# A fused two-block transformer step: transposed inputs from the host, splits on one engine, and a reordered second mixer

## The reference

```python
h = rmsnorm(x, mix_pre_g)                       # first block
u, v_s, q, k, v_a, g_a, g_b, f = split(h @ w_in)
y_a = spatial_gating(gelu(u), gelu(v_s), ...)
y_b = forgetting_attention(q, k, v_a, f, b_forget)
x = x + rmsnorm((sigmoid(g_a) * y_a + sigmoid(g_b) * y_b) @ w_out, mix_post_g)
x = x + rmsnorm(swiglu(rmsnorm(x, ffn_pre_g), w_gate, w_up, w_down), ffn_post_g)
proj = rmsnorm_2(x, norm_mix_g) @ w_in_2        # second block
x = x + concat(pool_mixer, mlstm_mixer, attn_mixer) @ w_out_2
x = x + mem_cross_attn(rmsnorm_2(x, norm_mem_g), mem, ca_wq, ca_wkv, ca_wo)
x = x + ec_moe(rmsnorm_2(x, norm_ffn_g), router_w, expert_w_gu, expert_w_down)
return rmsnorm_2(x, final_norm_g)
```

## Time and profile before

| | |
|---|---|
| median of 3 runs (lowest to highest) | 1486.63 us (1486.63 to 1488.58) |
| profiled execution | 1486.36 us, of which 1484.6 us are the profile's span |
| PE busy | 1147.1 us, 77% |
| DVE / ACT / POOL busy | 468.4 / 398.3 / 74.1 us |
| DMA | 503.33 MB, mean 339 GB/s |
| x and first products | to 25.3 us |
| first block | to about 426 us |
| second block with its mixer and router | to about 588 us |
| experts and final norm | to the end |

### The profile page before, as it was taken

The page is one execution under the profiler, slowest core; times in us unless marked ns, Lnnn a source line. Parts: engine busy times, 40 slices in busy tenths (PEclk is TensorE's granted clock), DMA queues, the critical chain, the costliest instruction groups (busy, mean ns, idle before and its releaser), DMA issues.

```text
span 1484.6 us, 19383 instructions
## 1 busy us (share of the span) xinstructions
PE 1147.1 (77%) x8336; PEld 754.3 (51%) x8336; DVE 468.4 (32%) x954; ACT 398.3 (27%) x890; POOL 74.1 (5%) x89
## 2 busy tenths in 40 slices
PE   9999999999999998995566466566665564565677
PEld 7888988888877875442322223223222232232234
DVE  6575777656788764110000000000000000000002
ACT  5665567555657642110000000000000000000002
POOL 0000020000035411000000000000000000000000
PEclk9999999999999998798778778787887787887789
DMA  8435546555553488999999999999999999999996
GB/s 313 171 138 203 198 172 223 208 207 199 199 187 114 149 347 343 397 436 434 433 437 426 433 433 435 424 442 430 430 437 426 438 430 433 433 426 440 423 424 288
DMA packets 29450, 503.33 MB, mean 339 GB/s; under 512 B 4275, under 2 KB 4915, under 8 KB 8245
## 3 DMA queue, kind: packets, MB, share of 16 engines
q1 hardware_dynamic: 25344, 493.43, 79.7%
q10 hardware_dynamic: 4020, 8.66, 1.6%
HBM read 501.03 MB, written 1.05 MB: 338 GB/s over the span
## 4 chain that ended last, share of the span: by engine, by line
issue 60%; PE 32%; DVE 5%; ACT 1%; POOL 1%; POOLq 0%; DVEq 0%; ACTq 0%
PE PB L378 9%; PE PB L358 5%; PE PB L359 5%; PE PB L360 5%; PE PB L379 4%; DVE SPL L1575 1%; DVE XN L1595 0%; PE PB L409 0%; POOL SP L2238 0%; PE PB L815 0%; PE PB L680 0%; PE PB L418 0%; PE PB L507 0%; PE PB L799 0%; PE PB L454 0%
## 5 line engine op out<-in xcount | busy, mean ns | idle before, releaser
L919 PE MATMUL PB<-RING,XS 128*32 128x512 f32 x2048 | 292.8, 720 | 177.0 <-DMA RING<-in_wgu_dram 176.7
L919 PEld LDWEIGHTS PB<-RING,XS 128*32 128x32 f32 x2048 | 68.4, 126 | 345.3 <-issue 249.8
L951 PE MATMUL PB<-RING,HHT 128*32 128x256 f32 x2048 | 150.9, 452 | 111.9 <-DMA RING<-in_wdn_dram 110.5
L1575 DVE TENSOR_TENSOR SPL<-RAW,SPH 128x512 fp32r<-128x512 f32 x318 | 207.0, 709 | 31.4 <-ACT SPH L1048 28.7
L378 PE MATMUL PB<-XT,SPH 128*128 128x512 f32 x544 | 194.1, 401 | 0.0
L1048 ACT ACTIVATE SPH<-RAW 128x512 fp32r<-128x512 f32 x340 | 186.8, 620 | 7.4 <-DMA RAW<-in_wst_dram 3.3
L951 PEld LDWEIGHTS PB<-RING,HHT 128*32 128x32 f32 x2048 | 75.3, 129 | 172.2 <-issue 141.7
L379 PE MATMUL PB<-XT,SPL 128*128 128x256 f32 x544 | 152.4, 280 | 0.0
L1506 ACT ACTIVATE SG<-PB 128x512 f32<-128x512 f32 x16 | 9.6, 597 | 506.1 <-PE PB L919 506.1
L2128 DVE SCALAR_TENSOR_TENSOR YL<-PB,COLS,YH 128x256 fp32r<-128x256 f32 x64 | 31.0, 484 | 279.0 <-ACT YH L1520 279.0
L378 PEld LDWEIGHTS PB<-XT,SPH 128*128 128x128 f32 x544 | 102.2, 188 | 24.6
(11 more groups left out here) (398 smaller groups left out, 1577.5 us busy)
## 6 DMA issues: line engine op xcount, KB each, us to landing
RAW<-in_wst_dram SPq DMA_DIRECT2D x84, 1024.0 KB, 4.9
RING<-in_wgu_dram SPq DMA_DIRECT2D x13, 2048.0 KB, 40.4
RING<-in_wgu_dram SPq DMA_DIRECT2D x4, 4096.0 KB, 22.3
RING<-in_wgu_dram SPq DMA_DIRECT2D x14, 1024.0 KB, 8.1
RING<-in_wdn_dram SPq DMA_DIRECT2D x6, 2048.0 KB, 13.4
RING<-in_wdn_dram SPq DMA_DIRECT2D x2, 4096.0 KB, 19.0
RING<-in_wdn_dram SPq DMA_DIRECT2D x3, 1024.0 KB, 41.0
RAW<-in_wst_dram SPq DMA_DIRECT2D x4, 256.0 KB, 5.6
```

What stands on the lines that cost most here:

```text
L919: i = e.matmul(PB[b][32 * c:32 * c + 32, :], XS[x % 2][:, k, :], chunk_at(n)[:, 512 * c:512 * c + 512], start=k == 0, stop=k == KD - 1)
L951: w = e.matmul(PB[b][32 * j:32 * j + 32, 0:T], HHT[:, j, 32 * c:32 * c + 32], chunk_at(n)[:, T * (4 * (c % 2) + j):T * (4 * (c % 2) + j + ...
L1575: e.tensor_tensor(l, src, h.bitcast(F32), ALU.subtract).then_inc(*lo.up())
```

## The change

1. The host also passes `xt`, x transposed, and the gain as a column for each of the eight feature blocks (GCOL). The transposes of x and the gain's spreading go. Both halves of VA come first (U_VA is now units 0 to 3), from x times gain without the row factor: XRH and XRL are split from `XR * GCOL`, the first 128 rows' first half straight on ACT and DVE (`high_first`, `low_first`), the other three quarters multiplied on POOL and then split. The row factor r is applied when VA is emptied (`scale=rn[...]`); for Q, K and all later products PE spreads r over PSUM bank 6 (`norm_factors`, in the second half of VA), DVE multiplies XR by it, and ACT and DVE split that into XTH and XTL. SP now issues unit 0, units 1 and 2, and only then x in rows, which only the sums of squares and the later residual use.
2. `mem` is passed transposed; PE's 16 transposes go and ACT and DVE split MEM as it lands.
3. `POOL_PIECES` is empty: all pieces are split by DVE.
4. In the second mixer `memory_values(0)` moves ahead of the loop (and of `pool_means`); the softmax division of turns 0 to 2 is made half by DVE and half by POOL; the scan's maxima are spread from rows 0 to 39 for odd heads and rows 64 to 103 for even ones, in turn with the scan's score matmuls (MS is copied to the lower rows by ACT); DVE's `low(4)` ahead of the loop becomes `low(6)` in turn 0, and ACT's `high(4)` ahead of it becomes `high(2)` behind the taps and `high(4)` at the end of turn 0.

```diff
-U_VA, U_Q, U_K = (0, 6), (2, 8), (4, 10)
+U_VA, U_Q, U_K = (0, 2), (4, 8), (6, 10)
-POOL_PIECES = (120, 121, 122, 123, 279, 283, 287, 293, 294, 295, 298, 299, 302, 303, 306, 307, 310, 311, 322, 327, 331, 335)
+POOL_PIECES = ()
...
         e.wait_ge(*gps.at("warm"))
-        for _ in range(7):
+        for _ in range(13):
             e.matmul(PB[4][:, 0:P], WARM[:, :], WARM[:, :], start=True, stop=True)
-        e.wait_ge(s_row, 16)
...
-        rtile(U_VA[0], 2, 0, [("xt_in", 0, j) for j in range(2)], ("va", 0, 0), between=second_tile)
-        rtile(U_VA[0], 3, 1, [("xt_in", 1, j) for j in range(2)], ("va", 0, 1))
+        def norm_factors():
+            e.wait_ge(s_id, 16)
+            for t in range(2):
+                e.wait_ge(*gps.at(("r", f"x{t}")))
+                r = e.matmul(PB[6][:, tiles[t]], rn[f"x{t}"].to_broadcast([P, P]), ident, start=True, stop=True)
+            r.then_inc(*mixd.up("r_in"))
+        for half_ in range(2):
+            for j in range(2):
...
+                    i = rk(U_VA[half_] + j, k, 4 * j + k, 2 - 2 * half_ + t, XRH, XRL, t, j + k == 0, j == 1 and k == 3)
...
+        free = {b: act.at(("va", int(b < 2), b % 2)) for b in range(4)}
+        for j in range(2):
+            e.wait_ge(*vec.at(("xt_in", j)))
...
-                for k in range(4 * j, 4 * j + 4):
-                    i = e.transpose(PB[b][:, (k % 4) * P:(k % 4 + 1) * P], MEM[:, t, k * P:(k + 1) * P], ident)
...
         def attn_turn(i):
-            if i < 3:
-                e.wait_ge(*gps.at(("attn_p", i)))
-            else:
-                e.wait_ge(*vec.at(("attn_p", i)))
             for j in range(2):
+                e.wait_ge(*(gps.at(("attn_p", i)) if j and i < 3 else vec.at(("attn_p", i))))
...
+            m = slice(0, 40) if h % 2 else slice(64, 104)
             for d in range(2):
                 g = 32 * d + h
-                i = e.matmul(PB[0][:, T * d:T * d + T], NEGI[64:104, g:g + 1].to_broadcast([40, P]), MS[64:104, :], start=True, stop=True)
+                i = e.matmul(PB[7][:, T - T * d:512 - T * d], QK[r, kb, d * P:d * P + P], QK[r, qb, :], start=True, stop=True)
...
+                i = e.matmul(PB[0][:, T * d:T * d + T], NEGI[m, g:g + 1].to_broadcast([40, P]), MS[m, :], start=True, stop=True)
...
+        memory_values(0)
         for i in range(4):
...
             if i >= 1:
                 attn_turn(i - 1)
-            memory_values(i)
-            if i >= 1:
+                memory_values(i)
                 scan_values(i - 1)
...
+            e.activation(XTH[:, 4 * j:4 * j + 4, :].rearrange("p k (t c) -> p k t c", t=2),
+                         XR[:, :, 4 * j:4 * j + 4, :].rearrange("p t k c -> p k t c"), ACT.Copy).then_inc(*act.up(("xt_in", j)))
         e.dma_start(WFR[:, :], io["wf"]).then_inc(s_wf, 16)
...
+        for t in range(2):
+            e.wait_ge(*gps.at(("r", f"x{t}")))
+        for t in range(2):
+            values_out(0, t)
+        high(8)
+        for t in range(2):
+            values_out(1, t)
         for half_ in range(2):
-            for t in range(2):
-                values_out(half_, t)
...
-            high((2, 4, 5, 5)[i])
+            high((4, 4, 5, 5)[i])
...
-            low((2, 4, 5, 5)[i])
+            low((6, 4, 5, 5)[i])
...
+        for t, j in ((1, 0), (0, 1), (1, 1), (0, 0)):
...
+            e.tensor_tensor(a, a, GCOL[:, 4 * j:4 * j + 4].unsqueeze(2).to_broadcast([P, 4, P]), ALU.mult).then_inc(*gps.up(("xg", t, j)))
...
+        for t in range(2):
+            e.dma_start(X[:, t, :], io["x"][t * P:(t + 1) * P, :]).then_inc(s_x[t], 16)
```

More of the change, by code:

```diff
@@ L267, in build @@
     s_first = [sem(f"s_first{q}") for q in range(4)]
+    s_next = [sem(f"s_next{i}") for i in range(2)]
     s_w = [sem(f"s_w{i}") for i in range(NRAW)]
@@ L497, in tensor @@
                 e.wait_ge(*free[bank])
-                rtile(U_VS + 2 * h, bank, t, [("xt_in", t, j) for j in range(2)], ("vs", h, t))
+                rtile(U_VS + 2 * h, bank, t, [("xt_in", j) for j in range(2)], ("vs", h, t))
                 free[bank] = act.at(("vs", t, h))
@@ L1098, in values_out @@
             bank = t if half_ else 2 + t
[L1099 removed]
+            e.activation(VA[:, t, halves[half_]], PB[bank][:, :], ACT.Copy, scale=rn[f"x{t}"]).then_inc(*act.up(("va", half_, t)))
         def joined(dst, bank, name, scale=1.0):
@@ L1205, in scalar @@
         e.wait_ge(*vec.at(("gu", 7)))
-        for t in range(2):
-            for j in range(2):
-                high_turned(t, j, 2 * t + j, MEMH, turn.at(("mem", t, j)), "memt")
+        e.wait_ge(s_mem, 16)
+        for q in range(4):
+            e.activation(MEMH[:, 2 * q:2 * q + 2, :], MEM[:, 2 * q:2 * q + 2, :], ACT.Copy).then_inc(*act.up(("memt", q)))
         post_squares(0, "po0", "out")
@@ new lines, in vector, with low_first @@
+        e.wait_ge(s_gcol, 16)
+        e.wait_ge(s_xt[0], 16)
+        def low_first(k):
+            e.wait_ge(*act.at(("xr0", k)))
+            e.scalar_tensor_tensor(out=XRL[:, k, 0:P], in0=XR[:, 0, k, :], scalar=GCOL[:, k:k + 1], in1=XRH[:, k, 0:P].bitcast(F32),
+                                   op0=ALU.mult, op1=ALU.subtract).then_inc(*vec.up(("xr0", k)))
+        low_first(0)
+        low(1)
+        for k in range(1, 4):
+            low_first(k)
+        low(1)
+        low_rows(1, 0)
@@ new lines, in vector @@
+        low(2)
+        low_rows(0, 1)
+        low_rows(1, 1)
+        low(8)
+        for t in range(2):
+            e.wait_ge(s_x[t], 16)
+            e.tensor_tensor_reduce(XN[:, t, halves[1]], X[:, t, halves[1]], X[:, t, halves[1]], 1.0 / D, 0.0, ALU.mult, ALU.add, ss[f"x{t}"][1]).then_inc(*vec.up())
+        for t in range(2):
+            mean_square(f"x{t}", act.at((f"x{t}", 0)), vec.so_far())
+        low(4)
+        e.wait_ge(*gps.at(("xg", 0, 0)))
+        e.wait_ge(*mixd.at("r_in"))
@@ L2235, in attn_norm @@
             e.wait_ge(*vec.at(("attn_r", i)))
-            for n in range(4):
+            for n in range(2, 4):
                 a = SP_[2 * (i % 2) + n // 2][:, n % 2 * T:n % 2 * T + T]
```

192 lines of the change are left out of this document (98 added, 94 removed).

## The result

The changed kernel takes 1489.78 us (median of 20 runs, 1487.73 to 1491.41), the kernel before, timed beside it, 1486.66 us (20 runs). The ratio is 1.0020 with a 95% interval of 1.0014 to 1.0026: **slower by 2.1 to 3.9 us**, where a gain of 1.1 us had been summed. The profiled execution of the changed kernel has a span of 1487.0 us, 2.4 more than before.

The account below looks back on a forecast made before the run. PE was taken to bound the front and weight transfers the experts. Head -3.0, memory +1.9, splits +1.5, mixer +0.3 and late +0.4 sum to +1.1 us gained: 1486.36 - 1.1 = 1485.3 us, range 1479.0 to 1490.5.

Parts of the forecast that it names:

- Regimes and transfer: Whole kernel: PE bounds the front, weight transfers the experts; time gained before the first expert product reaches the end whole.
- The start: Head: first product at about 6.5 us instead of 11.54, VA done at 31 to 32.5 us.
- What ends last in the head: Head: ACT's steps before emptying PB0, 11.7 us after XR, hold Q to 37.5 us; -1.3 against 36.2 before.
- Rival B: Head: ACT's issues don't hold VA's emptying, Q starts at 30 to 32 us; 1478.3 us, chance 0.15.
- The clock's term: Head: PE, idle before Q, restarts at the lower clock; 1.77 us lost, judged from a 1.58 us wait in the mixer.
- Head: Sum for the head, early start, Q's wait and clock: -3.0 us, bounds -5 to +4.5.
- Memory: Memory's 16 transposes leave PE, which has no wait there: +1.9 us, bounds 0 to 2.2.
- Splits ahead of the mixer: Splits on DVE only shorten PE's waits at 416.17 and 426.06 us: +1.5 us, bounds 0.5 to 2.2.
- Late: Pieces at 534.33 us, split by DVE alone, hold PE less: +0.4 us, bounds 0 and 0.5.
- The mixer: Second mixer: shorter PE waits against idle PE and more DVE pieces: +0.3 us, bounds -3.7 to +3.3.
- rival D: Mixer's first turn: six DVE pieces set the second maxima, PE idles; mixer -3.7 to -5, 1489.8 us, chance 0.13.
- Rival E: Head: POOL's four multiplications hold DVE's splits, r or XR after 28 us; 1488.0 us, chance 0.10.

Follow-up runs that it names:

- the first experiment: Changed kernel with, on ACT, the eight pieces right behind XTH, then all four VA banks emptied, the nine small transfers issued last: 1483.35 us, ratio 0.9975.
- the late POOL pieces: Kernel before with POOL's pieces 120 to 307 given to DVE, the six from the mixer on left on POOL: 1478.37 us in one run.

## Why the prediction was wrong, point by point

**Regimes and transfer: right.** PE works through most of the front, and the front's loss of 2.21 us at the first expert product is the span's 2.4.

**The start: wrong by 2 us and more.** Forecast 6.5 us; it came at 8.43, and PE then waited 1.24 us for the second product's operands and ran at about half clock to 14.2 us. I had taken the first quarter to land earlier than before; it was `xt` for which ACT waited last, to 6.64 us, against 6.65 before. Behind that landing stand two roundings on ACT and two differences on DVE, not "one product-sized step each", and the second product's low part stood behind three more differences. PE was done with VA at 34.1 us (39.42 - 5.33), not 31 to 32.5.

**What ends last in the head: the mechanism right, its start late.** From XR done to Q I summed 11.7 us; it is 11.06 (28.36 to 39.42). Rival B fell: the issues do hold the emptying. But XR was done at 28.36 us, not 25.5 to 26.5. The two small matmuls that spread r came at 25.29 us: POOL had r at 23.8 us, and they stood behind 60 products that the late start had moved. DVE would not have been ready much sooner: its pieces ended at 25.16 us, where I had them ready at 23, behind a wait of ACT for unit 3 of 1.36 us. DVE idled 0.85 us for the matmuls. The clock's term was 1.77 and is 2.4, behind 5.33 us of waiting. That 1.58 us of waiting brings the lower level each time, as I took it, the runs do not show: behind 1.50 us (the first experiment) and 1.57 us (the late POOL pieces) the clock stayed at 1.00. **Head: forecast -3.0, measured -5.6, beyond the bound of -5: Q 1.9 us later than summed, the clock 0.7 dearer.** The bound had DVE's pieces 2 us late, which they were, but not PE's start. This is the larger part of the error. That the head lost although its first product came 3.1 us earlier was the forecast.

**Memory: right.** +1.9 forecast, 2.0 measured. **Splits ahead of the mixer: right.** +1.5 forecast, 1.7 measured, 1.5 of it by the two waits named. **Late: right.** 0.4 and 0.5.

**The mixer: +0.3 forecast, -1.2 measured; its sum is the step that failed in mechanism.** The value lies within the bounds, but by terms that cancel: +3.5 from DVE's lead, -2.6 by the six pieces, -1.6 by `memory_values(0)` ahead of the scores, -0.2 by the divisions; they sum to -0.9, and 0.3 is left open with the spreading. Three things were wrong in it.

- *PE's idle time where `memory_values(0)` stood* is named in the prediction ("so PE idles there instead"), but the sum of the losses has only the clock for it. PE waits 3.27 us there, and putting the products back gave 1.6 us. Nor did I see that DVE's first maxima stand behind them.
- *The six pieces* had 0.61 us each, less 1.2 for the two that had left their place ahead of the first maxima. They took 0.97 each beside POOL's taps, and the two had freed nothing, since DVE then idled 3.82 us for the scores. That is rival D's mechanism: 2.6 us with the clock, where I had 1.2.
- *"From there to the mixer PE has no wait, and DVE's lead buys nothing."* PE has no wait there, but DVE goes into a stretch in which it is waited for, and its lead is worth 3.5 us at the mixer's end, the clock behind the transposes included. I looked for what PE waits for and stopped where PE did not wait; the engine that becomes the bound next had to be followed. This mistake alone would have made the kernel faster than forecast: it hid most of what the other two cost.

**Rival D** named 1489.8 us, and 1489.78 were measured. That is luck: it had 3.7 to 5 us lost in the mixer, which lost 1.2, and the rest is the head's.

**Rival E** was there too, and its sign (XR after 28 us) came true: DVE's pieces in the head beside POOL's multiplications take 1.07 us each, and 1.3 to 1.4 for the splits of XR. But r was ready 1.5 us before PE's small matmuls came, so it can have acted only through PE's start, where three differences took 1.66 us beside POOL's first multiplication (0.35 for the one ahead of it). No run took it away alone, so what it costs stays open. The range ended at 1490.5 and held the time, by the slower rivals; the side was wrong because two terms, head and mixer, were mis-sized by 2.6 and 1.5 us the same way.

## What to carry to other kernels

Issues of transfers are work of the engine whose list they stand in: nothing that another engine waits for should stand behind them. When an edit makes an engine faster that nobody waits for, follow it to the next place where somebody does, and price the lead there. A change of many parts is best priced by a run for each part: here one emptied table gains 5.7 us by its trace, and what came with it took more than that back.

## What the runs showed that was not expected

The first product of the head moves from trace to trace by as much as the whole effect: 9.63 to 11.55 us in four traces with the head of before, 8.2 to 11.3 in ten with the changed one or a form of it. Marks further on must be compared as stretches. And an engine's stated releaser can be the wrong one of several: Q's wait in the first experiment is put down to a DVE piece, while ACT's emptying ended 0.26 us ahead of it. A wait of some 1.5 us can cost as much again in clock or nothing: 1.58 us before and 1.57 with POOL's late pieces differ by 1.5 us behind them.
